# A two-block transformer kernel: the router's transposes read the residual itself, and its norm and shift are applied later

## The reference

```python
x = x + gate_mix[:, None, :] * (mixed @ w_out[layer])
h2 = _modulate(_rmsnorm(x, g_ffn[layer]), shift_ffn, scale_ffn)      # h * (1 + scale) + shift
y = _hierarchical_moe(h2, w_group, w_expert, w_gate, w_up, w_down)
x = x + gate_ffn[:, None, :] * y
# inside _hierarchical_moe, per token:
#   group  = argmax(h2 @ w_group)           (4 groups)
#   two best of the 8 experts of that group by h2 @ w_expert (32 experts in all)
#   y = sum of weight_e * (silu(h2 @ w_gate[e]) * (h2 @ w_up[e])) @ w_down[e]
```

## Time and profile before

| | us |
|---|---|
| median of 3 runs (lowest, highest) | 1050.97 (1048.11, 1051.05) |
| the profiled execution: its time | 1050.97 |
| the profiled execution: its span, first to last instruction | 1049.3 |
| PE busy | 987.7 (94%) |
| DVE busy | 568.7 (54%) |
| ACT busy | 340.3 (32%) |
| POOL busy | 76.9 (7%) |
| mean granted clock of TensorE, as a share of full speed | 0.979 |

### The profile page before, as it was taken

One profiled execution on the slowest core, in us unless ns is written; L12 is line 12 of the kernel. 1 busy time (PEld: TensorE's weight loads), 2 busy tenths in 40 slices (PEclk: granted clock), 3 DMA queues, 4 the chain that ended last, 5 costly groups with the idle time before them and its releaser, 6 DMA issues.

```text
span 1049.3 us, 15232 instructions
## 1 busy us (share of the span) xinstructions
PE 987.7 (94%) x5954; PEld 703.9 (67%) x5955; DVE 568.7 (54%) x960; ACT 340.3 (32%) x522; POOL 76.9 (7%) x112
## 2 busy tenths in 40 slices
PE   5997888999999999999978899999999999999996
PEld 5996788999999998898967544444444444444442
DVE  7668689899989985737684522221122221222223
ACT  5555646445445554526550210111011110011111
POOL 7200110111011200100001000000000000000000
PEclk9999989999999998799989999999999999999999
DMA  8334174888879754244244999999999999999994
GB/s 292 122 121 161 60 256 149 318 305 298 308 289 341 287 191 161 81 161 161 81 161 146 428 428 428 428 428 427 427 427 427 429 427 428 429 428 429 428 422 179
DMA packets 60086, 312.00 MB, mean 297 GB/s; under 512 B 3989, under 2 KB 5354, under 8 KB 47242
## 3 DMA queue, kind: packets, MB, share of 16 engines
q1 hardware_dynamic: 52320, 284.83, 67.3%
q0 software_dynamic: 7312, 26.39, 7.2%
q10 hardware_dynamic: 410, 0.16, 0.1%
HBM read 310.32 MB, written 1.05 MB: 297 GB/s over the span
## 4 chain that ended last, share of the span: by engine, by line
PE 84%; DVE 8%; DMA 4%; ACT 3%; issue 1%; POOL 1%; DVEq 0%; SPq 0%; ACTq 0%
PE bank L800 14%; PE bank L801 13%; PE bank L802 13%; PE bank L1183 10%; PE bank L1171 10%; PE bank L1210 9%; PE bank L1117 5%; DMA eslots<-in_w_gate 4%; PE bank L1133 3%; DVE ring_r L1592 1%; PE bank L885 1%; PE bank L854 1%; PE bank L789 1%; PE bank L1005 1%; ACT scratch L1493 1%
## 5 line engine op out<-in xcount | busy, mean ns | idle before, releaser
L800 PE MATMUL bank<-hT_r,ring_r 128*128 128x256 f32 x744 | 215.6, 290 | 7.8 <-DVE ring_r L1592 4.2
L802 PE MATMUL bank<-hT_r,ring_r 128*128 128x256 f32 x744 | 212.9, 286 | 0.0
L1592 DVE TENSOR_TENSOR ring_r<-ring,ring_r 128x2048 fp32r<-128x2048 f32 (+1 forms) x78 | 173.8, 2263 | 12.5 <-ACT ring_r L1278 11.9
L1278 ACT ACTIVATE ring_r<-ring 128x2048 fp32r<-128x2048 f32 (+1 forms) x78 | 144.2, 1889 | 39.7 <-DMA ring<-in_w_up 35.8
L800 PEld LDWEIGHTS bank<-hT_r,ring_r 128*128 128x128 f32 x744 | 145.2, 195 | 10.5 <-issue 8.7
L801 PE MATMUL bank<-v_tok_r,ring_r 128*128 128x256 f32 x512 | 145.6, 284 | 0.0
L802 PEld LDWEIGHTS bank<-hT_r,ring_r 128*128 128x128 f32 x744 | 145.2, 195 | 0.0
L1210 PE MATMUL bank<-eslots,scratch 128*64 128x512 f32 x512 | 113.4, 595 | 6.9 <-ACT scratch L1493 6.9
L1183 PE MATMUL bank<-eslots,scratch 128*64 128x512 f32 x512 | 113.3, 595 | 0.5 <-issue 0.5
L1171 PE MATMUL bank<-eslots,scratch 128*64 128x512 f32 x512 | 112.7, 592 | 0.6 <-DMA eslots<-in_w_gate 0.6
L2070 DVE TENSOR_TENSOR scratch<-scratch,bank 128x512 f32<-128x512 f32 x16 | 11.0, 688 | 181.1 <-PE bank L1183 181.1
(11 more groups left out here) (270 smaller groups left out, 1355.3 us busy)
## 6 DMA issues: line engine op xcount, KB each, us to landing
eslots<-in_w_gate SPq DMA_DIRECT2D x32, 2048.0 KB, 26.5
eslots<-in_w_up SPq DMA_DIRECT2D x30, 2048.0 KB, 23.7
eslots<-in_w_down SPq DMA_DIRECT2D x30, 2048.0 KB, 26.7
ring<-in_w_up SPq DMA_DIRECT2D x16, 2048.0 KB, 11.7
ring<-in_w_in SPq DMA_DIRECT2D x9, 2048.0 KB, 7.9
ring<-in_w_down SPq DMA_DIRECT2D x8, 2048.0 KB, 9.0
kT<-in_w_ada POOLq DMA_DIRECT2D x24, 512.0 KB, 7.7
ring<-in_w_out SPq DMA_DIRECT2D x4, 2048.0 KB, 8.4
```

Source lines behind the costliest of these rows:

```text
L800: pe.matmul(dst, lhs[0], rhs[0], start=start, stop=False, **flags)
L802: return pe.matmul(dst, lhs[1], rhs[0], start=False, stop=stop, **flags)
L1278: sc.activation(hi, raw, ACT.Copy).then_inc(s_whi, 1)
L1592: last = ve.tensor_tensor(lo, raw, hi, ALU.subtract)
```

## The change

The turn reads `x` as it stands, and the copies out of PSUM apply only the gain. The factor `r` is a scalar of each token, so it passes through the products: it is applied to the logits (one instruction for each tile in place of the copy into `lg`) and in ACT's copy back into `hn` (`scale=rstd`). The shift is left out of `hT` and comes in at two places. For the logits it is one row, the sum over the features of shift times router weight, made on DVE from a second copy of the router's weights (`wshift`, features in the order `8p + k`) and summed over the partitions by one matmul. For the experts it is added when a pair's tokens leave PSUM: four ACT and four DVE instructions of 128x128 with a bias in place of one of 128x512 on each. The columns of the shift are made in the order `8p + k`, by weight loads with a stride of 8 elements.

```diff
 # POOL
             pool.wait_ge(s_mixed, 1)
+            pool.dma_start(wshift[:, :, 0:NGRP], a["w_group_2"].rearrange("o (p k) n -> p (o k) n", p=P),
+                           allow_slow_non_contiguous=True).then_inc(s_wr, 16)
+            pool.dma_start(wshift[:, :, NGRP:NGRP + NEXP], a["w_expert_2"].rearrange("o (p k) n -> p (o k) n", p=P),
+                           allow_slow_non_contiguous=True).then_inc(s_wr, 16)
             pool.dma_start(wr[:, :, 0:NGRP], ...
             pool.dma_start(wr[:, :, NGRP:NGRP + NEXP], ...
 # PE, columns
-                        c = part * D + k * P
-                        last = pe.matmul(bank[:, n * KD + k:n * KD + k + 1], ada[:, c:c + P], ones[:, 0:1],
+                        rows = ada[:, part * D:(part + 1) * D]
+                        rows = rows.rearrange("q (p k) -> q k p", k=KD) if part == 3 else \
+                            rows.rearrange("q (k p) -> q k p", k=KD)
+                        last = pe.matmul(bank[:, n * KD + k:n * KD + k + 1], rows[:, k, :], ones[:, 0:1],
 # PE, router
-            turn("moe", hn)
-            pe.wait_ge(s_wr, 32)
+            turn("moe", x, range(T - 1))
+            pe.wait_ge(s_wshift, 1)
+            pe.matmul(PS[0][:, 0:NL], ones[:, :], shift_sum, start=True, stop=True).then_inc(s_wshift, 1)
+            turn("moe", x, range(T - 1, T))
+            pe.wait_ge(s_wr, 64)
...
-            pe.wait_ge(s_counts, 1)
+            pe.wait_ge(s_np, 1)
 # ACT
-            scaled("moe", lambda k: gffnc[:, k:k + 1], lambda k: modc[:, 2, k:k + 1])
+            scaled("moe", lambda k: gffnc[:, k:k + 1])
             for n in range(4):
                 sc.wait_ge(s_back, n + 1)
+                sc.wait_ge(s_rs, len(ROOTS) - 2 * T + n // 2 + 1)
...
-                sc.activation(dst, PS[n][:, :].rearrange("q (p k) -> q k p", k=KD), ACT.Copy).then_inc(s_h2, 1)
+                sc.activation(dst, PS[n][:, :].rearrange("q (p k) -> q k p", k=KD), ACT.Copy,
+                              scale=rstd[:, n // 2:n // 2 + 1]).then_inc(s_h2, 1)
 # ACT, tokens(p)
-                sc.activation(xeT[:, 0:4, :], PS[4][:, :].rearrange("p (a b) -> p a b", a=4), ACT.Copy)\
-                    .then_inc(s_xeA, 1)
+                for k in range(KD // 2):
+                    last = sc.activation(xeT[:, k, :], PS[4][:, k * P:(k + 1) * P], ACT.Identity, scale=1.0,
+                                         bias=modc[:, 2, k:k + 1])
+                last.then_inc(s_xeA, 1)
 # DVE, gated
-                    then(ve.tensor_tensor(x[:, t, half], x[:, t, half], mix[:, t, half], ALU.add))
+                    ins = ve.tensor_tensor(x[:, t, half], x[:, t, half], mix[:, t, half], ALU.add)
+                    if c == 0:
+                        then(ins)
+                    else:
+                        ins.then_inc(s_src["moe"], 1)
+                        ve.wait_ge(s_src["moe"], t + 1)
...
-                return root()
 # DVE, router
             ve.wait_ge(s_mod, 6)
+            ve.wait_ge(s_wr, 64)
+            then(ve.tensor_tensor(wshift, wshift, modc[:, 2, :].unsqueeze(2).broadcast_to([P, KD, NL]), ALU.mult))
+            ve.tensor_reduce(shift_sum, wshift.rearrange("p k n -> p n k"), X, ALU.add).then_inc(s_wshift, 1)
             for t in range(T):
-                r = gated(PROJ_BANKS[1], post_attn, t, s_proj[1])
-                ve.tensor_scalar(hn[:, t, :], x[:, t, :], r, None, ALU.mult).then_inc(s_src["moe"], 1)
-            scaled("moe", lambda k: gffnc[:, k:k + 1], lambda k: modc[:, 2, k:k + 1])
+                gated(PROJ_BANKS[1], post_attn, t, s_proj[1])
+            ve.wait_ge(s_wshift, 2)
+            ve.tensor_copy(shift_logits, PS[0][:, 0:NL]).then_inc(s_lgT, 1)
+            scaled("moe", lambda k: gffnc[:, k:k + 1])
...
-            then(ve.tensor_copy(lg, PS[5][:, 0:T * NL].rearrange("p (t n) -> p t n", t=T)))
+            for t in range(T):
+                last = ve.scalar_tensor_tensor(lg[:, t, :], PS[5][:, t * NL:(t + 1) * NL], root(), shift_logits,
+                                               ALU.mult, ALU.add)
+            then(last)
 # DVE, tokens(p)
-                ve.tensor_copy(xeT[:, 4:8, :], PS[5][:, :].rearrange("p (a b) -> p a b", a=4)).then_inc(s_xeV, 1)
+                for k in range(KD // 2, KD):
+                    c = (k - KD // 2) * P
+                    last = ve.tensor_scalar(xeT[:, k, :], PS[5][:, c:c + P], modc[:, 2, k:k + 1], None, ALU.add)
+                last.then_inc(s_xeV, 1)
```

More of the change, by code:

```diff
@@ L225, in two_block_kernel @@
         wr = piece(KD, NGRP + NEXP)
+        wshift = piece(KD, NGRP + NEXP)
+        shift_sum = piece(NGRP + NEXP)
+        shift_logits = piece(NGRP + NEXP)
         cmax, over = piece(1), piece(1)
@@ L359, in two_block_kernel @@
         s_h2 = sem("s_h2")
+        s_wshift = sem("s_wshift")
         s_lg = sem("s_lg")
@@ L363, in two_block_kernel @@
         s_lg2 = sem("s_lg2")
-        s_counts = sem("s_counts")
         s_r1 = sem("s_r1")
@@ L1080, in back @@
                 last.then_inc(s_back, 1)
+            pe.wait_ge(s_lgT, 1)
             back(0, 0)
-            pe.wait_ge(s_lgT, 1)
+            pe.wait_ge(s_lgT, 2)
             for t in range(T):
@@ L2095, in _ @@
             then(ve.tensor_reduce(cmax, PS[6][:, 0:NEXP], X, ALU.max))
-            ve.nop().then_inc(s_counts, 1)
             then(ve.tensor_scalar(over, cmax, float(SLOTS), float(PAIRS * (PASSES - 1)), ALU.is_gt, ALU.mult))
```

## The result

The changed kernel takes 1060.19 us (median of 3 runs, 1059.74 to 1065.17) against 1050.97 us: the ratio is 1.0097, with a 95% interval of 1.0061 to 1.0133. The forecast was 1055.0 us with a range of 1050 to 1059.5; the sign was right, the size was not. The same kernel, run again in the experiments, gives 1.0093 (1.0056 to 1.0129).

What follows compares the result with a forecast made beforehand. PE's chain and the expert-weight transfers both run at their limit, the loads catching PE at the end. Turn 2.6, logits 0.15, clock 0.5, columns 0.3, loop 1.5, less 1.0 idle: +4.0, 1055.0 us; range 1050 to 1059.5.

Steps and rivals of the forecast that it cites:

- Turn, +2.6: Router: DVE's wait for the fourth POOL transfer delays the residual, so PE's second turn starts 2.6 us later.
- Rival A: Router: transfers land early, the fourth by about 567, so not slower; 1051.3 us with the columns; chance 8%.
- Rival B: Router: small pieces are serial work, adding 3.3 us to the fourth landing, at 575.8; time 1058.3 us; chance 20%.
- Clock, +0.5: Router: PE's low clock reaches further into the logits; +0.5 us, between bounds of 0 and 2.4.
- logits, +0.15: Router logits: two instructions with a root in place of one copy; +0.15 us.
- Columns, +0.3: Column matmuls ahead of the router: 8 load weights at a 32-byte stride; +0.3 us, between 0 and 1.1.
- Loop, +1.5: Expert loop: DVE's four additions end past ACT's copy, 0.1 us a pair in 15 pairs; +1.5 us.
- Rival C: Expert loop: additions go by L1562, 0.32 us a pair, 4.8 in place of 1.5; time 1058.3 us; chance 22%.
- Idle time, -1.0: End of the expert loop: a later PE uses up its idle times of 0.47 and 0.57 us; -1.0 us.
- the rule behind it: Expert loop: an earlier PE brings nothing, as the last gate weights land at 1013.1 us; a later PE loses its idle time.
- The 0.47 us at 993.53: PE idle time near the loop's end, put down to a transfer's landing although the row calls it issue.

Runs made afterwards that it cites:

- experiment 1: Changed kernel with the two wshift loads issued some 130 us earlier, so DVE waits for 32 in place of 64: ratio 1.0008 to the kernel before.
- experiment 12: Changed kernel with DVE's wait, product and sum moved behind the residual and the turn's copies, loads issued when they were: ratio 1.0036 to the kernel before.
- experiment 4: Changed kernel with early wshift loads, DVE's four additions as one, and columns from contiguous weights (shift in another feature order): ratio 0.9986 to the kernel before.
- experiment 6: Changed kernel with early wshift loads, one DVE addition, and shift columns laid out anew by GpSimd for contiguous reads, right feature order: 1049.61 us, ratio 0.9994.
- experiment 7: As experiment 6, with the second block's projection finishing both tiles' first halves ahead of the second halves, freeing load slots sooner: 1047.99 us, ratio 0.9975.
- experiment 2: Changed kernel with DVE's four 128x128 additions made one 128x512 tensor_tensor with the shift broadcast: ratio 1.0053 to the kernel before.
- experiment 3: Changed kernel with the shift's columns made by contiguous weight loads, the shift standing in another feature order: ratio 1.0051 to the kernel before.
- experiment 9: Kernel before with only DVE's wait for all four transfers, product and sum put ahead of the residual, the sum unused: ratio 1.0076.
- experiment 10: Kernel before with only DVE's 128x512 token copy replaced by four 128x128 additions: ratio 1.0056.
- experiment 11: Kernel before with both parts of the late columns, 16 matmuls, made from weights at a stride of 8 elements: ratio 1.0052.

## Why the prediction was too low

The chain in the traces grew by 9.2 us for the 4.0 forecast: 2.0 of the missing 5.2 lie in the loop, 1.9 in and around the columns, 1.3 in the router. Step by step, by the terms of its sum:

- **Turn, +2.6: held.** +2.1 in this trace, +2.2 in the first. The mechanism is the one described, seen in the chain above, and taken away by experiments 1 and 12. The fourth landing was 7.6 us after the issue for 8.2, the product and the sum took 1.1 us to the next start for 0.9. The rule of the Trainium skill (DMA: Bandwidth & Descriptors, anatomy of one DMA, SWDGE path), which gives some 2.3 us for such a transfer, is contradicted by every trace here: 7.5 to 8.4 us beside the loads of expert weights, 3.7 to 4.7 where they are not running (experiments 1, 4, 6 and 7). Rival A falls with it. Rival B falls as well: two transfers more did not slow the fourth, and its small pieces take no 8 us by themselves; the traces put the difference down to what else is being loaded, though no run varied that alone.
- **Clock, +0.5, and logits, +0.15: low.** What is left of the router behind the turn is +2.4 us in this trace and 1.2 on average, for 0.65. The whole router comes out right on average only because the turn was put 0.4 too high: it costs 26.43 and 26.28 us in the two traces of the changed kernel, 24.57 and 24.20 in experiments 2 and 3, whose router is the same; and 21.92, 20.94 and 23.12 in the three traces with the router of before. The means, 25.4 and 22.0, differ by 3.4 us; the forecast's three terms come to 3.25. What differs inside each set is the stretch at 1.2 GHz; its second fall, under the dispatch, has no term in the sum.
- **Columns, +0.3: the first term that failed.** It is 1.9 us at full clock (experiments 1 and 3), beyond the upper bound of 1.1. The bound took 0.14 us for one matmul. But the 32 instructions of the row are 16 matmuls, two instructions each, so a contiguous matmul takes about 0.23 us and a strided one twice that. The 4.54 us also had 2 us at 1.2 GHz in it, which the prediction did not say. The Trainium skill (SBUF — State Buffer, the note on cachelines) gave the sign and no price; the trace gives 0.24 us more for each matmul with a strided 128x128 load.
- **Loop, +1.5: the second.** It is +3.5. The four additions take 1.13 us, the lower end of what was forecast, and end 0.09 us past ACT, also as forecast (0.1). What was missing is the way from that end to the product: 0.21 us for 0.06 before, as PE's wait for the weights now comes behind DVE's end and no longer beside ACT's copy. 0.09 and 0.15 make 0.25 a pair, in 14 pairs; that the 0.15 is this instruction is read from the traces, and no run took it away by itself. Rival C had nearly the size (0.32) and the wrong reason. The working of the four additions was also off: 0.477 and 0.537 less 0.17, and less 0.1 between starts, are 0.21 to 0.27 between starts and 0.31 to 0.37 for the last, together 0.92 to 1.16 us and not 1.1 to 1.35. Measured are 0.26 and 0.34, so that the 1.13 lies in both.
- **Idle time, -1.0: held**, and so did the rule behind it: experiments 4, 6 and 7 show that the stream of loads sets the end as soon as PE is earlier. The 0.47 us at 993.53, which the prediction put down to a transfer against its row, is one: the last piece of a load lands at 993.44.

With 1.9 for 0.3 and 3.5 for 1.5 the sum is 3.25 + 1.9 + 3.5 - 1.0 = 7.65 us, and with the router of these two traces 8.9. The range was too narrow, because two costs with an unknown price were each put near their lower bound and added.

What reading `x` brings once that wait is out of the way is a router of 18.6 us in place of 20.9 to 23.1; the wait in front of the residual costs 5.6 to 7.9 us in the changed kernel, and experiments 1 and 12 take that back in two different ways. Open is why single edits measure 0.1 to 0.3% more than their traces show (experiments 3 and 9 to 12); why the clock falls a second time, under the dispatch, in some traces and not in others, was not tried.

## What to carry to other kernels

A wait for data that is needed late belongs where the data is needed: on an engine that works in order, all behind it pays, here 6 to 8 us for a sum that fits into idle time a few instructions later. When an engine takes over the last place ahead of a wait, count not only its end but also what the waiting engine still has to do between that wait and its work, times the number of rounds: an instruction that was hidden beside the old last one is hidden no longer. And where a stream of loads runs at its limit beside the engine, ask for every gain whether it also starts the stream earlier: 3 us on PE alone brought nothing to speak of, and two loads issued 2.5 us earlier brought 2.7 in the traces and 1.6 in the medians.

## What the runs showed of the hardware

- Eight weight loads of 128x128 at a stride of 32 bytes add 1.9 us, sixteen 3.9 us, to matmuls of one column: 0.24 us each, on top of about 0.23. The strided ones take the same 0.238 us per instruction at 1.2 and at 2.4 GHz (two instructions a matmul), the others 0.213 and 0.112.
- A GpSimd transfer of 128 KB in small pieces lands 3.7 to 4.7 us after its issue with next to nothing else being loaded, 7.5 to 8.4 us beside the loads of expert weights; one of 16 KB after 2.9 to 3.5 and about 8.
- PE starts 0.05 to 0.06 us after the end of the instruction that it waits for, be it ACT's or DVE's, and 0.21 us after it where a semaphore instruction of its own queue comes in between (in two of the loop's 14 such rounds both are 0.12 to 0.17 longer).
- DVE reading PSUM: one 128x512 addition with a broadcast operand takes 0.69 us, as the copy did; four 128x128 additions with a scalar take 1.13. ACT's four with a bias take 1.14 for 0.60.
- With the same code of the router and the same idle time of 3.29 us ahead of them, PE's transposes ran at 2.4 GHz in one execution (experiment 10: 1.09 us, then logits 2.19) and at 1.2 GHz in another (experiment 11: 1.97, then 3.64). A single trace fixes the cost of such a pause to no better than 2 us.
